# Old states as the stationary operand in a hybrid decoder step: one change, read before it was run

## What is computed

```python
def gdn_chunk(S, inp):
    q, k, v, g, beta = inp
    G = jnp.cumsum(g, axis=-1)
    ...
    sol = lax.linalg.triangular_solve(M, rhs, left_side=True, lower=True, unit_diagonal=True)
    value, kcd = sol[..., :dv], sol[..., dv:]
    v_new = value - jnp.einsum('bhld,bhdv->bhlv', kcd, S)
    qk = jnp.einsum('bhtd,bhjd->bhtj', q, k) * dec_incl
    o = jnp.einsum('bhld,bhdv->bhlv', q * jnp.exp(G)[..., None], S) + jnp.einsum('bhtj,bhjv->bhtv', qk, v_new)
    S_new = S * jnp.exp(GL)[..., None] + jnp.einsum('bhjd,bhjv->bhdv', k * jnp.exp(GL - G)[..., None], v_new)
    return S_new, o
```

## Time and profile before

| | |
|---|---|
| median of 3 runs | 1010.77 us |
| lowest and highest | 1004.40, 1012.48 us |
| the profiled execution's own time | 1007.93 us |
| its span, first to last instruction | 1006.2 us |
| mean granted TensorE clock in it | 0.926 of 2.4 GHz |

### The profile page before, as it was taken

How to read it: one execution, slowest core, us unless ns; L and a number is a source line. 1 busy time by engine, 2 the same in 40 slices (tenths; PEclk the granted TensorE clock), 3 DMA queues, 4 the chain that set the end, 5 groups by cost and what they waited for, 6 DMA issues and landing times. The chain is left out here.

```text
span 1006.2 us, 16374 instructions
## 1 busy us (share of the span) xinstructions
PE 918.8 (91%) x6874; PEld 764.8 (76%) x6874; DVE 429.0 (43%) x718; ACT 299.4 (30%) x608; POOL 257.2 (26%) x266
## 2 busy tenths in 40 slices
PE   8999989897999699867988999999799999999984
PEld 7988868897989588745557999999799666666551
DVE  4687864444224531154336743166334222222223
ACT  5676553230112343211025643433210000000002
POOL 8311326554242200024215500565500000000000
PEclk7999999998797598988779999999999999999997
DMA  8834014000002781300345444544048999999991
GB/s 222 271 123 127 1 49 133 1 1 1 2 1 84 237 283 54 118 1 1 122 150 149 125 152 156 168 166 132 39 167 351 423 420 420 420 419 421 421 384 50
DMA packets 97767, 175.21 MB, mean 174 GB/s; under 512 B 8948, under 2 KB 84308, under 8 KB 85349
## 3 DMA queue, kind: packets, MB, share of 16 engines
q1 hardware_dynamic: 97688, 174.09, 48.2%
HBM read 163.13 MB, written 10.95 MB: 173 GB/s over the span
## 5 line engine op out<-in xcount | busy, mean ns | idle before, releaser
L272 PE MATMUL ps<-rounded,rounded 128*128 128x304 f32 x632 | 196.2, 310 | 13.5 <-DVE rounded L260 9.5
L274 PE MATMUL ps<-rounded,rounded 128*128 128x304 f32 x632 | 192.0, 304 | 0.0
L273 PE MATMUL ps<-hL,rounded 128*128 128x304 f32 x504 | 153.4, 304 | 0.0
L272 PEld LDWEIGHTS ps<-rounded,rounded 128*128 128x128 f32 x632 | 120.2, 190 | 22.5 <-DVE rounded L260 9.7
L274 PEld LDWEIGHTS ps<-rounded,rounded 128*128 128x128 f32 x632 | 120.4, 190 | 0.0
L260 DVE TENSOR_TENSOR rounded<-ring,rounded 128x2048 fp32r<-128x2048 f32 x36 | 84.0, 2332 | 73.2 <-ACT rounded L254 72.6
L254 ACT ACTIVATE rounded<-ring 128x2048 fp32r<-128x2048 f32 x48 | 91.2, 1909 | 26.7 <-PE ps L274 16.2
L273 PEld LDWEIGHTS ps<-hL,rounded 128*128 128x128 f32 x504 | 96.3, 191 | 0.4 <-issue 0.2
L260 POOL TENSOR_TENSOR rounded<-ring,rounded 128x2048 fp32r<-128x2048 f32 x12 | 55.2, 4601 | 89.4 <-ACT rounded L254 89.2
L1085 PE MATMUL ps<-arena 128*128 128x128 f32 (+1 forms) x576 | 64.7, 277 | 1.6 <-DVE arena L1005 1.3
L1085 PEld LDWEIGHTS ps<-arena 128*128 128x128 f32 (+1 forms) x576 | 62.2, 192 | 3.2 <-DVE arena L1005 1.9
(11 more groups left out here) (377 smaller groups left out, 1765.6 us busy)
## 6 DMA issues: line engine op xcount, KB each, us to landing
ring<-in_w_in SPq DMA_DIRECT2D x36, 1024.0 KB, 5.7
ring<-in_expert_w_gate SPq DMA_DIRECT2D x16, 1024.0 KB, 20.8
ring<-in_expert_w_up SPq DMA_DIRECT2D x16, 1024.0 KB, 15.9
ring<-in_expert_w_down SPq DMA_DIRECT2D x16, 1024.0 KB, 23.4
arena<-in_expert_w_down SPq DMA_DIRECT2D x12, 1024.0 KB, 21.2
arena<-in_expert_w_gate SPq DMA_DIRECT2D x12, 1024.0 KB, 21.5
arena<-in_expert_w_up SPq DMA_DIRECT2D x12, 1024.0 KB, 24.5
arena<-in_state_gla SPq DMA_DIRECT2D x4, 1024.0 KB, 7.4
```

The lines of the kernel that those rows point to most:

```text
L272: self.nc.tensor.matmul(self.psum[b][:, 0:NT], h[:, j, c], xh(j), start=(j == 0), stop=False)
L273: self.nc.tensor.matmul(self.psum[b][:, 0:NT], h[:, j, c], xl(j), start=False, stop=False)
L274: ins = self.nc.tensor.matmul(self.psum[b][:, 0:NT], lo[:, j, c], xh(j), start=False, stop=(j == KB - 1))
```

## The change

In the third chunk the operands of the old-state matmuls change places. The state is stationary (128x128); moving are the columns of a segment alone, its keys and its decayed queries together: for that POOL copies the keys behind the decayed queries into `bEG` (column 64 on), once a half, and `halves` picks the same columns of both parts. No mask is needed, and one pass of 9 matmuls a head serves keys and queries. The products land transposed, channels on partitions. ACT copies them to SBUF, PE turns the key part for the residual (four transposes a half), and the query part stays as it is: PE computes the attention part of the outputs in the same orientation, and DVE adds the two into `oaT`. `MT`, `SEGM`, both `SEGM` loops, the copy and the turn of the outputs go. The updates stay as they are.

In the freed ring slots 2 and 3 lies `HQ`: ACT and DVE split slabs 12 and 13 there during the third chunk. `gla` begins with the high parts of slabs 14 and 15 and takes slabs 12 and 13 from `HQ`. Since slabs 18 and 19 use slots 2 and 3, SP issues their loads only when the blocks of slabs 12 and 13 are done, and the two small parameter loads come first.

```diff
@@ Core @@
+        self.HQ = [self.rounded("ring", SW * p, SW) for p in (2, 3)]
@@ delta, POOL @@
-            if c == 1:
-                segment_mask(nc, pl, MT, s["mt_ready"])
-            if c == 2:
-                for h in range(8):
-                    nc.gpsimd.tensor_tensor(SEGM[:, h, :, :], bc_mid(KT[:, h, 256:NT], 9), MT[:, :, :], ALU.mult).then_inc(s["ktm_ready"], 1)
...
+                if c == 2:
+                    nc.gpsimd.tensor_copy(w[bEG][:, :, 64:64 + l], KT[:, hs, 256:NT]).then_inc(s["kc_ready"], 1)
...
-                for h in range(8):
-                    hh = h // 4
-                    pl.wait_ge(s["ks_done"], 3 + hh)
-                    pl.wait_ge(s["qe_ready"], 5 + hh)
-                    nc.gpsimd.tensor_tensor(SEGM[:, h, :, :], bc_mid(buf[hh][bEG][:, h % 4, 0:l], 9), MT[:, :, :],
-                                            ALU.mult).then_inc(s["qm_ready"], 1)
@@ delta, ACT @@
+            else:
+                for n in range(2):
+                    core.high_part(act, N_QB + n, core.HQ, core.HQ[n])
+                for hh in range(2):
+                    act.wait_ge(s["old_done"], hh + 1)
+                    nc.scalar.activation(buf[hh][bB][:, :, 0:64 + l], bank4(4 * hh + 2, 64 + l), ACT.Copy).then_inc(s["kst_ready"], 1)
...
-                    act.wait_ge(s["o_done"], i + 1)
-                    nc.scalar.activation(w[bB][0:l, :, :], bank4(b0 + 2, 128)[0:l], ACT.Copy).then_inc(s["otok_ready"], 1)
-                    act.wait_ge(s["otok_done"], hh + 1)
-                    nc.scalar.activation(oaT[:, hs, T0[c]:T0[c] + l], bank4(b0 + 2, l), ACT.Copy).then_inc(s["oT_ready"], 1)
@@ delta, DVE @@
+                for n in range(2):
+                    core.low_part(dve, nc.vector, N_QB + n, core.HQ, core.HQ[n])
                 residual(0)
...
                 for hh in range(2):
+                    dve.wait_ge(s["o_done"], 5 + hh)
+                    nc.vector.tensor_tensor(oaT[:, 4 * hh:4 * hh + 4, 256:NT], bank4(4 * hh + 2, l), buf[hh][bB][:, :, 0:l], ALU.add).then_inc(s["oT_ready"], 1)
@@ delta, PE @@
-                def old_states(b, hh, stop):
+                def halves(ap, q):
+                    cols = slice(0, TAIL) if q == 0 else slice(TAIL + TS * (q - 1), TAIL + TS * q)
+                    return ap.rearrange("p (w t) -> p w t", w=2)[:, :, cols]
+                for hh in range(2):
+                    pe.wait_ge(s["y4_ready"], 5 + hh)
+                    pe.wait_ge(s["qe_ready"], 5 + hh)
+                    pe.wait_ge(s["kc_ready"], 1 + hh)
+                    if hh == 0:
+                        pe.wait_ge(s["sa_in"], 16 * 8)
                     for h in range(4):
                         for q in range(9):
                             st = S[:, 4 * hh + h, :] if q == 0 else sample_state(4 * hh + h)[:, q - 1, :]
-                            ins = mm(bank4(b, 128)[0:l, h, :], SEGM[:, 4 * hh + h, q, :], st, start=(q == 0), stop=(stop and q == 8))
-                        if not stop:
-                            ins = mm(bank4(b, 128)[0:l, h, :], buf[hh][bAT][0:l, h, 0:l], buf[hh][bDT][0:l, h, :], start=False, stop=True)
-                    return ins
-                pe.wait_ge(s["ktm_ready"], 8)
+                            ins = mm(halves(bank4(4 * hh + 2, 128)[:, h, :], q), st, halves(buf[hh][bEG][:, h, :], q), start=True, stop=True)
+                    ins.then_inc(s["old_done"], 1)
                 for hh in range(2):
-                    pe.wait_ge(s["y4_ready"], 5 + hh)
-                    if hh == 0:
-                        pe.wait_ge(s["sa_in"], 16 * 8)
-                    old_states(4 * hh, hh, True).then_inc(s["ks_done"], 1)
+                    pe.wait_ge(s["kst_ready"], hh + 1)
+                    for h in range(4):
+                        ins = tr(bank4(4 * hh, 128)[0:l, h, :], buf[hh][bB][:, h, 64:64 + l], 128)
+                    ins.then_inc(s["ks_done"], 1)
                 values(0)
                 values(1)
...
-                    pe.wait_ge(s["qm_ready"], 4 * hh + 4)
-                    old_states(b0 + 2, hh, False).then_inc(s["o_done"], 1)
+                    for h in range(4):
+                        ins = mm(bank4(b0 + 2, l)[:, h, :], w[bDT][0:l, h, :], w[bAT][0:l, h, 0:l], start=True, stop=True)
+                    ins.then_inc(s["o_done"], 1)
...
-                        if h == 1:
-                            pe.wait_ge(s["otok_ready"], hh + 1)
-                            for g in range(4):
-                                ins = tr(bank4(b0 + 2, l)[:, g, :], w[bB][0:l, g, :], l)
-                            ins.then_inc(s["otok_done"], 1)
@@ gla, SP @@
-        for n in range(N_VB, N_Z):
-            k.load_w(sp, n)
         sp.dma_start(UP[32:48, :], i_["gla_gate_up"][0]).then_inc(s["up_in"], 16)
         sp.dma_start(GB[32:33, :], i_["gla_gate_bias"]).then_inc(s["up_in"], 16)
+        for n in range(N_VB, N_Z):
+            if n >= N_VB + 2:
+                sp.wait_ge(unit_done, units(n - N_VB - 2 + N_QB + 1))
+            k.load_w(sp, n)
@@ gla, ACT @@
-        for n in range(N_QB, N_QB + 3):
-            k.high_part(act, n, HI)
+        for n in range(N_QB + 2, N_QB + 4):
+            k.high_part(act, n, HI, HI[n % 3])
...
-            if b % 2:
-                k.high_part(act, N_QB + b // 2 + 3, HI)
+            if b == 1:
+                k.high_part(act, N_VB, HI, HI[N_VB % 3])
+            if b in (5, 7):
+                k.high_part(act, N_VB + b // 2 - 1, HI)
@@ gla, DVE @@
-        for n in range(N_QB, N_Z - 1):
-            k.low_part(dve, nc.vector, n, HI)
+        for n in range(N_QB + 2, N_Z - 1):
+            k.low_part(dve, nc.vector, n, HI, HI[n % 3])
@@ gla, PE @@
-            k.block_of_slot(pe, N_QB + b // 2, b % 2, b % 4, HI)
+            k.block_of_slot(pe, N_QB + b // 2, b % 2, b % 4, k.HQ if b < 4 else HI)
```

More of the change, by code:

```diff
@@ L817, in delta @@
 def delta(k):
+    core = k
     nc, i_, o_ = k.nc, k.i_, k.o_
@@ L836, in delta @@
     SB = k.shaped(free[:, 0:4096], (4, 8, 128))
-    MT = k.shaped(free[:, 4096:4096 + 9 * L[2]], (9, L[2]))
-    SEGM = k.shaped(free[:, 4096 + 9 * L[2]:4096 + 81 * L[2]], (8, 9, L[2]))
-    assert 4096 + 81 * L[2] <= 4 * SW
     def sample_state(h):
@@ L847, in delta @@
         b4_ready p8_done y3_ready d8_ready p9_done y4_ready lz_done z_ready x_ready lw_done y_ready ks_done
-        mt_ready ktm_ready qm_ready otok_ready otok_done r_ready vn_done vn_ready o_done oT_ready ds_done s_ready kdm_ready kdo_ready su_done su_ready
+        kc_ready old_done kst_ready r_ready vn_done vn_ready o_done oT_ready ds_done s_ready kdm_ready kdo_ready su_done su_ready
         sa_in dve_c""")
```

## The result

| | before | after |
|---|---|---|
| median, runs of the comparison | 1010.63 us (20) | 1004.19 us (20) |
| lowest and highest | 1003.51, 1014.69 | 999.03, 1008.54 |
| the profiled execution, its span | 1007.93, 1006.2 | 1004.32, 1002.4 |

The ratio is 0.9941, 95% interval 0.9922 to 0.9960: 6 us faster, where 0.8 us slower was forecast (1011.6). The time lies outside the forecast's own range (1006 to 1017), and in the wider one for 8 in 10 (996 to 1020) only on the wrong side of no change.

The account below looks back on a forecast made before the run. PE, busy 91% of the span, was taken as the bound, at 1.2 GHz in the changed part. The delta stage ends 4.9 us later, the head start saves 4.1: +0.8, so 1010.8 becomes 1011.6 us; own range 1006 to 1017, 8-in-10 range 996 to 1020.

Parts of the forecast that it names:

- Old-state record at 0.213 us, clock at 0.50 throughout: Third chunk's 144 old-state records at 0.213 us each, 30.7 us; PE at 1.2 GHz from 256.6 us until the next stage's matmuls.
- clock up: Rival: the clock rises with the old states, which take 16.0 us; -25.7 in all, 986 us; chance 0.08.
- only the updates: Rival: only the third chunk's state updates get the higher clock; -7 to -14, 1001 us; chance 0.06.
- A load takes the same at either clock: Rival: weight loads equally long at 1.2 and 2.4 GHz, old states 144 x 0.111; -14.7, 997 us; chance 0.04.
- The two-piece moving operand: Slower rival: this operand costs each old-state record 0.075 us more at 1.2 GHz; +10.8, 1022 us; chance 0.09.
- Chain 7.9: After the old states: turn, DVE's residual, values of both halves and first half's outputs, 7.9 us; bounds 5 and 11.
- Updates and outputs 32.4: Third chunk's state updates for 8 heads, 30.7 us at 0.213 a record, plus second half's outputs, 1.7.
- Tail 3.9: End of the third chunk after the last matmuls: landing 0.4, DVE 2.1 and 1.4, together 3.9 us.
- POOL's copy +0.5: The keys' copy ahead of POOL's masks for each half; one copy delays PE, 0.5 us, bounds 0 and 0.6.
- Head start -4.1: Next stage's first matmul no longer waits for a high part (1.9) and a low part (2.3): -4.1 us.
- SP's order, nothing: Two of four weight loads after the border wait for HQ blocks: costs nothing, or one landing, 5.7 us, without cover.
- POOL's dropped masks, -0.3: Second chunk: masks ran beside DVE's L1033 (1.22 us, some 0.9 without them), so dropping them saves 0.3 us.

Follow-up runs that it names:

- the 128 rows: Changed kernel with the third chunk's state updates summed over all 128 partitions (rows 48 to 127 zeros): 996.12 us, ratio to before 0.9864.
- rows_wide_lift: Changed kernel with 128-partition updates, old-state moving operands of 40 to 128 columns, and twelve unused full-width matmuls ahead of the old states: 989.83 us; second run 990.38, ratio 0.9803.
- rows_lift: Changed kernel with 128-partition updates and twelve unused full-width matmuls ahead of the old states, moving columns still 8 and 32: 1002.35 us, ratio to before 0.9919.
- rows_wide: Changed kernel with 128-partition updates and old-state moving operands widened to 40 to 128 columns, no added matmuls: ratio to before 0.9887.

## Why the prediction was right and where it was wrong

- *Old-state record at 0.213 us, clock at 0.50 throughout*: right, 30.69 us; the clock was down from 255.01 to 347.17. The rival "clock up" and "only the updates" didn't come, and the lift with wide operands and the 128 rows show two ways in which it comes up. "A load takes the same at either clock" fell: 144 records took 16 us at 1.00 and 30.7 at 0.50. The two-piece moving operand pays nothing.
- *Chain 7.9*: 7.89. *Updates and outputs 32.4*: 32.31. *Tail 3.9*: 3.96.
- *POOL's copy +0.5*: 0.34 us long, and PE waited 0.29 for POOL's L882. The price came from L905, an operation with two operands; a copy is shorter.
- *Head start -4.1*: -4.3 in the profile; the moved parts are hidden, PE full in the old states. In the medians the changed kernel is no slower without it (0.9946 for 0.9942). *SP's order, nothing*: PE's idle time in `gla` is 18.5 us before and 18.5 after.
- *POOL's dropped masks, -0.3*: this is the step that failed. It was the term of the sum that was mis-sized; the two chunks took 2.5 to 3.8 us less in the profiles of the table, and 2.8 by the rows of the second chunk. Three things were missed. The addition alone takes 0.69, not 0.9. The second addition, 1.50 us, was not looked at: the copy, priced only as a delay of PE in the third chunk, also changes who comes first in the second. And a gap of PE was priced at its own length, while behind it the clock fell: 1.23 us of gap carried 1.53 of clock. With 2.8 in place of 0.3 the same sum gives 1009.1 us: the right sign, and a quarter of the measured 6 us.
- *The other 5 us, a term put at nothing*: the sum left every stage that the change doesn't touch as it was. Its base was right (1010.8 for 1010.63), but the clock moves in those stages too, and a median of this kernel answered to a shift of 1.5 us by 13. That the remainder is of this kind is argued from the experiments, not shown. The range, 996 to 1020, took it in by luck, through rivals that did not come.

## What to carry to other kernels

When an edit removes or adds work on POOL, list every DVE instruction with two SBUF operands beside it, before and after, in each place where the work stood; a 0.3 us copy may decide which of the two waits. Price a gap of PE with the time at 1.2 GHz behind it, read from the clock's stretches, and give it as a range: gaps of 1.5 to 2.7 us were followed here by nothing, 3.4 or 6.8 us of it. And where the clock falls often, take two or more profiles and both directions (undo the part, do it alone) before a difference under 1% is given a cause.

## What the runs showed of the hardware that was not expected

- 71 us of almost full PE (70.3 busy) at 0.50 without a rise, with 8 and 32 moving columns and then 48-row operands.
- The same old-state matmuls stayed at 1.00 with 40 to 128 moving columns (`rows_wide_lift`, 16.00 us) and fell to 0.50 with 8 and 32 (`rows_lift`); but with 40 to 128 they did not rise by themselves (`rows_wide`, 30.70 us at 0.50).
- A pause of 1.5 us at a stage's start made the kernel 12 to 14 us slower (994.62 and 996.70 to 1008.44), by some 30 us more at 1.2 GHz.
- A DVE addition of 128x512 with both operands in SBUF took 0.69 us alone and 1.22 and 1.50 beside POOL; where it was first, POOL's 1.04 became 1.48.
